# Unread identity products in TensorE's waits, and another order of work between the expert layer and the projection behind it

## The reference, cut to what matters

```python
h = rmsnorm(x, g_attn_norm); proj = h @ w_in
out_a = mixer_dilated(q_a, k_a, v_a, rel_bias)
out_b = mixer_mla(c_q, c_kv, k_rope, ...)
x = x + concat(rmsnorm(out_a, g_out_a), rmsnorm(out_b, g_out_b)) @ w_out
y = hierarchical_moe(rmsnorm(x, g_ffn_norm), ...)  # 32 experts, 2 per token
x = rmsnorm(x + y, g_final)
# even layer: retention and stick breaking, then mix
proj = rms_norm(x, pre_norm_w_2[0]) @ even_w_in_2
# odd layer: gated linear attention (hgrn2) and an LRU, then mix
proj = rms_norm(x, pre_norm_w_2[1]) @ odd_w_in_2
```

## Time and profile before

| | before |
|---|---|
| runs shown, us | 2508.58, 2507.5, 2494.13 (median 2507.5) |
| profiled execution, us | 2502.44 |
| its span, first to last instruction | 2500.6 |
| mean granted TensorE clock | 0.928 |
| TensorE busy | 2152.1 us, 86% |
| VectorE, ScalarE, GpSimd busy | 1335.4, 1095.8, 562.4 us |
| DMA | 399.70 MB, mean 160 GB/s |

### The profile page before, as it was taken

The page is one execution under the profiler, slowest core; times in us unless marked ns, Lnnn a source line. Parts: engine busy times, 40 slices in busy tenths (PEclk is TensorE's granted clock), DMA queues, the critical chain, the costliest instruction groups (busy, mean ns, idle before and its releaser), DMA issues. The chain is left out here.

```text
span 2500.6 us, 33467 instructions
## 1 busy us (share of the span) xinstructions
PE 2152.1 (86%) x11860; PEld 1770.9 (71%) x11860; DVE 1335.4 (53%) x2212; ACT 1095.8 (44%) x2028; POOL 562.4 (22%) x598
## 2 busy tenths in 40 slices
PE   6996897899798599999299999688788899966768
PEld 5885787789786466766278888578777677855657
DVE  3342665688654666666451210667675343428843
ACT  3232554678632355554351110256543333328641
POOL 1003100723011121322110000456521000017821
PEclk9998998999899699999699999889989899987889
DMA  4686865643253599996563221453152533141152
GB/s 158 199 249 172 239 189 141 182 90 67 71 184 125 210 361 371 356 343 260 202 219 122 80 80 47 133 135 72 50 197 84 156 129 128 67 143 53 44 194 93
DMA packets 216899, 399.70 MB, mean 160 GB/s; under 512 B 90560, under 2 KB 111424, under 8 KB 204080
## 3 DMA queue, kind: packets, MB, share of 16 engines
q1 hardware_dynamic: 177184, 315.04, 39.7%
q10 hardware_dynamic: 28384, 61.62, 6.5%
q0 software_dynamic: 11184, 21.13, 2.4%
HBM read 300.68 MB, written 114.85 MB: 166 GB/s over the span
## 5 line engine op out<-in xcount | busy, mean ns | idle before, releaser
L78 PE MATMUL pe_acc<-pe_w,hT 128*128 128x512 f32 x960 | 228.3, 400 | 5.3 <-DVE hT L724 5.3
L78 PEld LDWEIGHTS pe_acc<-pe_w,hT 128*128 128x128 f32 x960 | 183.7, 192 | 47.0 <-DVE hT L724 5.7
L78 PE MATMUL ex_gu<-hT,ex_xT 128*128 128x512 f32 x792 | 194.9, 402 | 0.8 <-DVE hT L2563 0.8
L2563 DVE TENSOR_TENSOR hT<-ex_raw,hT 128x2048 fp32r<-128x2048 f32 x66 | 150.9, 2288 | 83.3 <-ACT hT L2534 83.3
L78 PE MATMUL pg_acc<-hT,pg_w 128*128 128x512 f32 x768 | 179.7, 395 | 9.7 <-DVE pg_w L263 9.7
L78 PEld LDWEIGHTS pg_acc<-hT,pg_w 128*128 128x128 f32 x768 | 145.4, 189 | 43.0 <-DVE pg_w L263 10.1
L78 PEld LDWEIGHTS ex_gu<-hT,ex_xT 128*128 128x128 f32 x792 | 147.7, 190 | 34.8 <-DVE hT L2563 1.2
L2534 ACT ACTIVATE hT<-ex_raw 128x2048 fp32r<-128x2048 f32 x66 | 126.2, 1914 | 37.8 <-PEq L47 23.8
L302 DVE COPY pe_o<-pe_acc 128x512 f32<-128x512 f32 x28 | 19.3, 690 | 212.6 <-PE pe_acc L78 212.6
L2492 PE MATMUL ex_dn<-ex_wd,ex_hT 128*128 128x512 f32 x264 | 118.8, 593 | 0.8 <-ACT ex_hT L2528 0.8
L78 PE MATMUL pa_acc<-hT,pa_w 128*128 128x512 f32 (+1 forms) x432 | 100.5, 392 | 1.7 <-DVE pa_o L296 1.6
(11 more groups left out here) (504 smaller groups left out, 5184.0 us busy)
## 6 DMA issues: line engine op xcount, KB each, us to landing
ex_raw<-in_w_gate SPq DMA_DIRECT2D x33, 1024.0 KB, 7.4
ex_raw<-in_w_up SPq DMA_DIRECT2D x33, 1024.0 KB, 11.0
ex_wd<-in_w_down SPq DMA_DIRECT2D x33, 1024.0 KB, 14.1
pe_raw<-in_even_w_in SPq DMA_DIRECT2D x6, 2048.0 KB, 8.6
pg_raw<-in_odd_w_in SPq DMA_DIRECT2D x5, 2048.0 KB, 9.4
scr_q<-pa_o SPq DMA_DIRECT2D x32, 256.0 KB, 3.9
scr_k<-pa_o SPq DMA_DIRECT2D x32, 256.0 KB, 3.8
hT<-scr_k SPq DMA_DIRECT2D x16, 512.0 KB, 6.7
```

The lines of the kernel that those rows point to most:

```text
L78: mm = pe.matmul(out, a(p, k), b(q, k), start=(k == 0 and i == 0), stop=(k == n - 1 and i == 2))
L2563: dve.tensor_tensor(split(s, LO)[:, :, g, :], raw[:, s % NW, g, :].rearrange("p (k n) -> p k n", k=8), split(s, HI)[:, :, g, :].bitcast(F3 ...
```

## The change

A function `keep_clock` issues n products of a 128x128 identity matrix with itself, in float32, into a PSUM bank whose content nobody reads. It is called ahead of waits of TensorE: in `project` 14 before the wait for tile 0's load, 4 after it and 12 behind the first turn in `pa`; 22 after the load in `pe`; 14 at the start of `pg`; 32 at the start of `aa`, 12 at its end; 8 at steps 2 and 3 and 12 at the end of `ab`; 8 in `am`, 14 in `em` and `om` at the start, 14 and 6 before the last two turns of `em`; 24 and 36 in the router; 16 at the experts' start; 12 at the start of retention; 12 at the start and 12 at the end of stick breaking; 14 at two chunks of hgrn2.

In `project` the turn of tile j+1 moves from before the product of tile j into it, before its step k = 4, for j = 1 to 6. In `pe` ACT and DVE cut weight chunk 0 before they begin with the tiles, and at step 2 their work on tile 1's sum comes ahead of the cut of tile 0.

Between experts and `pe`: the buffer `ex_raw` outlives the experts' stage, and a new class `Ahead` lays the first buffers of `pe` into it. SyncE issues the loads of gain and weight chunk 0 when the last but one experts' weights have been cut, and those of the residual rows of tiles 0 and 1 and of g_final when the last have been. SyncE and not GpSimd waits for the scatters; GpSimd reads the block count two steps earlier and waits for scatters only where there are further blocks. `ExpertWeights` has no stage of its own any more.

```diff
+def keep_clock(pe, bank, ident, n):
+    for _ in range(n):
+        pe.matmul(bank[:, 0:P], ident[:, :], ident[:, :], start=True, stop=True, skip_group_check=True)
...
 (project, tensor)
+                if r:
+                    if wait_clock[0]:
+                        keep_clock(pe, r.tp[0], ident, wait_clock[0])
+                    r.loaded(pe, 0)
+                    keep_clock(pe, r.tp[0], ident, wait_clock[1])
+                else:
+                    keep_clock(pe, acc[0], ident, wait_clock[0])
...
                         if r and g == 0:
-                            for t in range(j + 1 if j else 0, min(j + 2, NT) if j else 1):
+                            for t in range(1 if j == 0 else 0):
                                 r.pe_turn(pe, t)
-                                if small and t in (5, 6):
-                                    small.tensor(pe, t - 5)
+                                keep_clock(pe, acc[1], ident, wait_clock[2])
...
+                        if r and g == 0 and 1 <= j < NT - 1:
+                            def before(k):
+                                if k == 4:
+                                    r.pe_turn(pe, j + 1)
+                                    if small and j + 1 in (5, 6):
+                                        small.tensor(pe, j - 4)
...
 (project, scalar)
+                if ahead:
+                    gains(act)
+                    split_hi(act, 0)
...
 (mix_out, tensor)
+                if order[0] == 0:
+                    f.loaded(pe, 0)
+                keep_clock(pe, acc[1], ident, 14 if f.gate else 8)
                 first_tile(pe)
                 for s in range(3, STEPS):
+                    if b.hT is not None and not tl and s >= STEPS - 2:
+                        keep_clock(pe, f.tp[0], ident, (14, 6)[s - STEPS + 2])
...
 (aa, tensor)
                 pe.wait_ge(keys_ok, 4)
+                keep_clock(pe, tps[0], ident, 32)
...
 (ab, tensor)
+                    if isinstance(T, int) and T in (2, 3):
+                        keep_clock(pe, pvs, ident, 8)
...
 (route, tensor)
+                pe.wait_ge(e_ready, 1)
+                keep_clock(pe, pd, ident, 24)
                 pe.wait_ge(m_ready, 1)
...
+                keep_clock(pe, pd, ident, 36)
                 pe.wait_ge(col_ok, 2)
...
 (experts, sync)
+                sp.wait_ge(w_lo, 2 * (BLOCKS - 1))
+                ahead.load_weights(sp)
+                sp.wait_ge(w_lo, 2 * BLOCKS)
+                ahead.load_rows(sp)
...
+                sp.wait_ge(stored[0], 16 * ((BLOCKS + 1) // 2))
+                sp.wait_ge(stored[1], 16 * (BLOCKS // 2))
...
 (experts, gpsimd)
+                    if s == BLOCKS + 2:
+                        n = blocks(pool)
...
-                pool.wait_ge(stored[0], 16 * ((BLOCKS + 1) // 2))
-                pool.wait_ge(stored[1], 16 * (BLOCKS // 2))
-                pool.sem_inc(free, 1)
...
-            with stage(nc) as st:
-                weights = ExpertWeights(st, A)
+            raw = routing.enter_context(nc.sbuf_tensor("ex_raw", [P, NW, 2, 8 * FF], F32))
+            ahead = Ahead(nc, raw, ...)
+            with ExitStack() as expert:
+                weights = ExpertWeights(nc, expert, A, raw)
```

More of the change, by code:

```diff
@@ L133, in project @@
         cuts = [sum(groups(c) for c in chunks[:g] if "split" in c) for g in range(N)]
-        gcol = st.sb(name + "_g", [P, nk]) if gain is not None else None
+        gcol = ahead.gcol if ahead else st.sb(name + "_g", [P, nk]) if gain is not None else None
         acc = [st.ps(f"{name}_acc{j}", [P, BANK]) for j in range(ring)]
-        gain_in = st.sem(name + "_gain_in")
+        gain_in = ahead.gain_in if ahead else st.sem(name + "_gain_in")
         raw_in = [st.sem(f"{name}_raw_in{s}") for s in range(nraw)]
-        k_in = [st.sem(f"{name}_k_in{k}") for k in range(nk)] if by_k else None
+        k_in = ahead.k_in if ahead else [st.sem(f"{name}_k_in{k}") for k in range(nk)] if by_k else None
         hi_ok, lo_ok = st.sem(name + "_hi_ok"), st.sem(name + "_lo_ok")
@@ L173, in _ @@
                         small.load(sp)
-                if gain is not None:
+                if gain is not None and not ahead:
                     for k0, v in gain:
@@ L184, in _ @@
                         (dst, src), = ch["load"]
-                        for k in range(nk):
+                        for k in range(0 if ahead else nk):
                             sp.dma_start(raw[:, 0, k, dst], src[:, k, :]).then_inc(k_in[k], 16)
@@ L258, in split_lo @@
                     dve.wait_ge(raw_in[g % nraw], 16 * sum(loads[g % nraw:g + 1:nraw]))
-                for k in range(ks[g][1]):
+                for k in range(a, min(b, ks[g][1])):
                     if not loads[g]:
@@ L333, in _ @@
                                 r.act_z(act, 0)
-                            gains(act)
-                            split_hi(act, 0)
+                            if not ahead:
+                                gains(act)
+                                split_hi(act, 0)
                             if not lx:
@@ L473, in __init__ @@
         self.junk = None if junk_in_z or expert_rows else sb("_junk", (P, width))
-        self.y = sb("_y") if expert_rows else None
-        self.e = [sb(f"_e{c}") for c in range(2)] if expert_rows else None
+        self.y = [given.y if given and u == 0 else sb(f"_y{u}", (P, width)) for u in range(ns)] if expert_rows else None
+        self.e = given.e if given and expert_rows else [sb(f"_e{c}") for c in range(2)] if expert_rows else None
         self.zrow = sb("_zrow", (P, width)) if z_gain is not None else None
@@ L483, in __init__ @@
         self.half = sb("_half", (P, 1))
-        self.prow = sb("_prow", (P, width)) if post is not None else None
+        self.prow = given.prow if given and post is not None else sb("_prow", (P, width)) if post is not None else None
         self.nt = ns // 2
@@ L487, in __init__ @@
         sem = lambda n: st.sem(name + n)
-        self.post_in, self.half_ok = sem("_post_in"), sem("_half_ok")
+        self.post_in, self.half_ok = given.post_in if given and post is not None else sem("_post_in"), sem("_half_ok")
         self.zrow_in = sem("_zrow_in")
@@ L533, in load @@
                 self.z_done(sp, t - self.ns)
-        for c0, w, src in self.loads:
+        for c0, w, src in self.loads if not self.given or t >= 2 else []:
             sp.dma_start(self.x[:, u, c0:c0 + w], src(t)).then_inc(self.tile_in[u], 16)
@@ L540, in load @@
                 sp.dma_start(self.e[c][:, u, :], rows(self.expert_rows[0], c * NT + t)).then_inc(self.tile_in[u], 16)
-        if t == 0 and self.post is not None:
+        if t == 0 and self.post is not None and not self.given:
             sp.dma_start(self.prow[:, :], self.post.partition_broadcast(P)).then_inc(self.post_in, 16)
@@ L2356, in half_by_parity, with experts @@
     return ap.rearrange("p (j k) -> p k j", k=2)
-def experts(nc, ident, xn, A, hT, idx, y, over, weights):
+def experts(nc, ident, xn, A, hT, idx, y, over, weights, ahead):
     raw, wd, xg, gu_in, wd_in = weights.raw, weights.wd, weights.xg, weights.gu_in, weights.wd_in
```

128 lines of the change are left out of this document (94 added, 34 removed).

## The result

The changed kernel takes 2492.03 us (median of 20 runs, 2486.2 to 2499.29) against 2504.39 (20 runs of the kernel before): ratio 0.9947, 95% interval 0.9938 to 0.9957, so by the ratio 13 us or 0.5% faster. The forecast was 34 us faster, and 2492.03 lies just outside its range. The profiled execution took 2491.72 us, its span 2489.9, at a mean granted clock of 0.949 against 0.928.

A forecast was written before the change was run, and what follows sets the result against it. TensorE, busy 86% of the span, was taken as the bound, losing time to waits and half-clock matmuls. From 2502.4 us, −5.8 −1.8 −4 −2.5 −1.7 −7.3 −11.3 = −34.4 gave 2468 us, range 2452 to 2492.

The forecast's parts named there:

- The passage: Between experts and pe: earlier stage start, early loads and reordered ACT and DVE work, −11.3 us, bounds −16 and −5.
- Part (1): Passage, stage start: GpSimd's 5.52 us drain is branch code fetch (4.5 earlier) or the scatters' end (0.9); taken as −3.9 us.
- Part (2): Passage, pe's start: rows and weights already there, chunk 0 cut in the loads' shadow, first product 3.1 us earlier.
- Part (3): Passage, pe's second product: x(1) ahead of tile 0's turn, −5.2 us, to some 12.4 behind the first; nothing from tile 2 on.
- Turns amid the products: In pa and pe, turning tile j+1 amid product j leaves TensorE's sum; chunk 1's cut comes later, +1.5 and +0.9 us.
- The clock: Across the stages, unread products before TensorE's waits keep its clock up, so half-clock work speeds up: −23 us together.
- rival A: The clock falls all the same, bare gaps stay, clock terms come to about −2; only the passage left: 2489 us, chance 0.13.
- the term of its row products: Router: the 16 row products gain 3.5 us from a higher clock.
- 65 us: TensorE's work in thirteen lowered-clock stretches: ceiling of what unread products can bring, less where another engine paces them.
- ab (−4 forecast): Stage ab: the second stretch's work at full clock gains 3.8 us and the twelve score products more; 2 paid; range −6 to 0.
- The overruns: Added products outlasting the waits they fill: router 1 us, aa 1.3, ab 2 paid, stick breaking 0.5 to 3.1.
- rival D: Slower: all blocks run at half clock and overrun their waits, 24.8 us against a passage of only −5: 2522 us, chance 0.06.

The follow-up runs named there:

- Experiment 5: Changed kernel with turns ahead of the products, the branch for further expert blocks (beyond 33) taken out on all engines: ratio 0.9948 to the kernel before, 2489.3 us.

## Why the prediction was wrong

**The passage: right in size, its first part for a wrong reason.** Forecast −11.3, measured 11. Part (1) −3.9, measured −4.1 (7.7 us for 11.9), but for neither of the two reasons. The text chose between a fetch behind the branch and the scatters' landing. Experiment 5 excludes the fetch. The landing falls by the trace of after: SyncE had passed its wait for the scatters and drained at 1194.8, GpSimd's drain ran on until 1197.5. The drain takes 5.5 to 6.7 us once GpSimd's indirect DMAs are behind it, whether it starts at the scatter or 4.6 us later; the gain is that it now runs beside the scatters' landing and not behind it. The sign that the prediction named, a last drain under 1 us, did not come (6.18). That the sum was met is luck in part. What the drain waits for stays open. Part (2) −3.1, measured −3.6. Part (3) −5.2, measured −5.6 at the second product (12.0 us behind the first), of which only 3.9 are the order of ACT's and DVE's work: with the turns ahead it is 13.7, and moving the turns alone gave 16.0 for 17.6. At chunk 1 nothing of it is left in after: "nothing gained" for the tiles from 2 on should have read "the gain is given back", since the tiles that ACT and DVE pace at 7 to 9 us end when these two end (that they do is argued, not shown by a run). Over eleven profiles with passage and turns ahead 1.9 us of it is kept on average (65.3 us from the first product to chunk 1, 67.2 in the one profile of before), which is within the spread of 64.1 to 67.7.

**Turns amid the products: sign right, too kind.** They stood as a neutral step with the later cut of chunk 1 behind it, +1.5 in pa and +0.9 in pe. Measured +2 to +5 together, 1.4 to 3.9 in pa's stage; in pe 1.5 at its end, against 1.7 gained at the second product, so that the net of pe is not resolved (65.6 and 67.2 us from the first product to chunk 1 with the turns amid, 64.1 to 67.7 with them ahead). The cover behind the turn was put at nothing; k = 1, 4 and 6 show it as a dose: 0.9926, 0.9947, 0.9991.

**The clock: −23 forecast, −5 to −7 measured. This is the step that failed.** It was written "what is gained is half of the work in that stretch". Two things are wrong in it.

First, rival A in most places: the clock was at half again for the work that counts, and in am the unread products themselves ran at half. The block filled the first wait, but between it and the long product there is a second (turn, ACT, DVE: 1.7 to 3.3 us), and behind it the product ran as slowly as before in pe, the experts and em in every profile, and in most in am and hgrn2. With this gap filled it ran at full clock at the experts' start and in pe. The router, with 0.39 us between block and product in after, was the exception, and the term of its row products is the one that held there: 3.5 forecast, 3.3 measured; over the twelve profiles it is 0.6 to 3.3, by the gap. The rule named in the prediction ("TensorE: Matmul & The Clock Gate" of the Trainium skill, on the second failure mode: short gaps, repeated, make the clock swing) is what the trace of after agrees with: mean clocks of 0.57 to 0.77 in those stretches, neither 0.50 nor 1.00. The measured time, 2492, lies 3 us from rival A's 2489, which had been given 0.13.

Second, and this would have sunk most of the sum even at full clock: the work is not what paces those places. With the second gaps filled the ratio is 0.9933, the mean of the two measurements without them (0.9913, 0.9953). Pe shows it best: 2.5 us less for the product, and the second product no earlier. In am some 1 to 2 of the 2.5 us came where the product was fast. The prediction said of its 65 us "less where another engine paces them", named hgrn2 and retention, and then credited em, pe, ab and aa. In ab (−4 forecast) the first twelve products still follow at 0.43 us in the trace of after, the gap of 4.8 us at the barrier being bare, and the stage took 243.5 to 246.2 us with or without blocks.

The overruns were in the forecast's sum for aa, ab, stick breaking and the router and not for retention, where real work starts 1.5 us later against the stage's start than before (9.2 and 7.7 us). Shortening the blocks of aa, retention, stick breaking and the experts gave nothing that the ratio shows, so these were not the loss that rival D feared.

The likeliest version after all this is the change with the turns ahead of the products: 0.9913 and 0.9953, with the second gaps filled 0.9933. These medians, 2486 to 2489 us, are below that of the change, by less than the intervals settle.

## What to carry to other kernels

A stretch at half clock is worth half of its work only where TensorE's own work is what the next engine waits for: before pricing it, follow the first long product to who waits for it, and see whether that one has been waiting. A block of unread products has to reach right up to the product that counts; a block with another wait behind it raises the mean clock and, here in most places, not the speed. One profile does not tell whether it did: am's first product took 7.76 to 9.30 us with the same block and the same gap of 2.37 us. When a preparing step moves into the middle of a product, what is left of the product behind it must cover what the other engines do behind it (here 2.6 us in pa and 3.4 to 4.5 in pe), or it becomes a wait for each tile.

## What the runs showed of the hardware that was not expected

GpSimd's drain behind its last indirect DMA takes 5.5, 6.2 or 6.7 us, without a branch before it and with the scatters landed or not; where the engine's last instruction was an ordinary vector operation, its drain ended 0.07 us behind it (nine drains in the trace of after), and behind a plain DMA that GpSimd issues in aa it ended 5.1 us behind (3.0 in the trace of before). TensorE's 3.8 us at the end of the experts' block lie over its last eight matmuls (3.67 us) and are shown at whatever comes next in its instruction list: the branch, or, without one, the drain. And stages whose code is untouched differ by up to 10 us between the profiles (aa 206 to 216), while whole runs of one kernel differ by about 0.5% (after: 2486.2 to 2499.29 us). A difference between two profiles of one execution each therefore says little of a stage.
